# A recurrence unit in another order: the next unit's factors made first, the substitution split and moved ahead of the fifth level, three filler products removed

## What is computed

```python
def step(state, inp):                       # one head, one token
    r_t, w_t, k_t, v_t, kk_t, a_t = inp
    sa = einsum('bhij,bhj->bhi', state, -kk_t)
    state = (state * w_t[:, :, None, :] + sa[..., :, None] * (kk_t * a_t)[:, :, None, :]
             + v_t[..., :, None] * k_t[:, :, None, :])
    y = einsum('bhij,bhj->bhi', state, r_t)
    return state, y
```

## Time and profile before

| | |
|---|---|
| median of 3 runs | 1934.21 us (1932.78 to 1935.5) |
| the profiled execution | 1931.3 us, its span 1929.5 us |
| mean granted TensorE clock | 0.967 of full speed |
| TensorE matmuls busy | 1812.6 us, 94% of the span |
| VectorE, ScalarE, GpSimd busy | 676.8, 446.8, 71.6 us |
| the eight units, first z to the last unit's end | 228.22 to 498.60 us, 270.4 us |

### The profile page before, as it was taken

One profiled execution on the slowest core, in us unless ns is written; L12 is line 12 of the kernel. 1 busy time (PEld: TensorE's weight loads), 2 busy tenths in 40 slices (PEclk: granted clock), 3 DMA queues, 4 the chain that ended last, 5 costly groups with the idle time before them and its releaser, 6 DMA issues.

```text
span 1929.5 us, 22747 instructions
## 1 busy us (share of the span) xinstructions
PE 1812.6 (94%) x9052; PEld 880.3 (46%) x9052; DVE 676.8 (35%) x1285; ACT 446.8 (23%) x924; POOL 71.6 (4%) x110
## 2 busy tenths in 40 slices
PE   6999999999898999999999989778989999999998
PEld 3434478878554333333333344676543333333333
DVE  3159687776324111111111245673241111111114
ACT  3284323223421111111111132452111111111111
POOL 4130000000000000000000200000000000000001
PEclk9999899999998999999999999887989999999999
DMA  8000000001242999999999872100049999999997
GB/s 294 6 0 1 1 1 2 2 1 45 88 174 88 376 427 430 428 428 429 429 428 429 352 270 87 44 1 1 0 174 396 429 428 429 429 429 429 427 429 295
DMA packets 68230, 460.95 MB, mean 239 GB/s; under 512 B 18700, under 2 KB 19846, under 8 KB 43590
## 3 DMA queue, kind: packets, MB, share of 16 engines
q1 hardware_dynamic: 56118, 435.90, 54.4%
q10 hardware_dynamic: 9744, 15.77, 2.2%
q0 software_dynamic: 2304, 8.39, 1.3%
HBM read 442.21 MB, written 17.83 MB: 238 GB/s over the span
## 4 chain that ended last, share of the span: by engine, by line
PE 80%; DVE 10%; ACT 5%; issue 2%; DMA 2%; SPq 0%; POOL 0%; DVEq 0%; ACTq 0%; POOLq 0%
PE bank L713 21%; PE bank L739 12%; PE bank L687 11%; PE bank L1969 5%; PE bank L936 4%; PE bank L1015 3%; PE bank L2260 3%; PE bank L695 2%; ACT hT L459 2%; PE bank L2105 2%; PE bank L2114 1%; PE bank L2096 1%; PE bank L1001 1%; PE bank L273 1%; PE bank L1952 1%
## 5 line engine op out<-in xcount | busy, mean ns | idle before, releaser
L713 PE MATMUL bank<-ring,arena 128*64 128x512 f32 x2048 | 450.4, 592 | 1.6 <-DVE arena L539 1.6
L606 DVE TENSOR_TENSOR arena<-arena,bank 64x512 f32<-64x512 f32 x64 | 68.3, 1067 | 626.0 <-ACT arena L467 625.9
L713 PEld LDWEIGHTS bank<-ring,arena 128*64 128x64 f32 x2048 | 146.8, 137 | 293.4 <-issue 291.3
L687 PE MATMUL bank<-arena 128*64 128x512 f32 x1024 | 234.1, 599 | 7.3 <-DVE arena L606 4.9
L739 PE MATMUL bank<-ring,arena 128*64 128x512 f32 x1024 | 239.4, 610 | 0.9 <-ACT arena L471 0.9
L1969 PE MATMUL bank<-hT,ring 128*128 128x512 f32 x336 | 147.8, 600 | 5.7 <-ACT arena L1425 4.0
L687 PEld LDWEIGHTS bank<-arena 128*64 128x64 f32 x1024 | 73.8, 138 | 155.2 <-issue 128.8
L467 ACT ACTIVATE arena<-bank 64x512 f32<-64x512 f32 x64 | 37.9, 592 | 401.1 <-PE bank L713 401.1
L739 PEld LDWEIGHTS bank<-ring,arena 128*64 128x64 f32 x1024 | 69.2, 139 | 125.7 <-issue 124.5
L539 DVE TENSOR_TENSOR arena<-bank,gffn 128x512 f32<-128x512 f32 x64 | 44.3, 692 | 187.1 <-PE bank L695 187.1
L1969 PEld LDWEIGHTS bank<-hT,ring 128*128 128x128 f32 x336 | 64.3, 192 | 87.9 <-issue 87.9
(11 more groups left out here) (368 smaller groups left out, 1977.4 us busy)
## 6 DMA issues: line engine op xcount, KB each, us to landing
ring<-in_moe_w_gate_dram SPq DMA_DIRECT2D x64, 2048.0 KB, 10.3
ring<-in_moe_w_up_dram SPq DMA_DIRECT2D x64, 2048.0 KB, 15.0
ring<-in_moe_w_down_dram SPq DMA_DIRECT2D x64, 2048.0 KB, 12.5
expert_rows<-arena ACTq DMA_DIRECT2D x120, 128.0 KB, 8.2
ring<-in_rec_w_in_dram SPq DMA_DIRECT2D x5, 2048.0 KB, 12.8
ring<-in_att_w_in_dram SPq DMA_DIRECT2D x3, 2048.0 KB, 8.6
ring<-in_rec_w_out_dram SPq DMA_DIRECT2D x2, 2048.0 KB, 8.4
ring<-in_att_w_out_dram SPq DMA_DIRECT2D x2, 2048.0 KB, 19.2
```

The costliest lines, as they stand in the source:

```text
L606: nc.vector.tensor_tensor(hb[0:CAP, par, :].rearrange("s (f p) -> s p f", f=4), sg[0:CAP, par, :].rearrange("s (p f) -> s p f", f=4), bank ...
L687: mm = nc.tensor.matmul(bank[2][h * CAP:(h + 1) * CAP, :], onehot[:, par, t, :], xm[:, t, h * 512:(h + 1) * 512], start=(t == 0), stop=(t ...
L713: mm = nc.tensor.matmul(bank[par][k * CAP:(k + 1) * CAP, :], xg[:, par, c, :], W[k][:, c * FF:(c + 1) * FF], start=(c == 0), stop=(c == KC ...
```

## The change

The order of the steps inside a unit is another one on three engines. On TensorE `first_products` of the next unit comes after t 3 (in the place of rest 1), `spread_rows` after outputs 0 (in the place of rest 3), and rest 1, 2 and 3 come after z 4, rhs 1 and z 5. The filler products `spin(3, 0)` of each unit are gone. On VectorE parts 3 to 5 of `prepare` come straight after the masks of level 3; the next unit's masks, its masked M and its rows follow level 3's sums; `block_inverse` is split in `substitute`, after level 4's sums, and `blocks_out`, after level 5's masks. On ScalarE a new copy, `rows_copy`, takes the spread rows from bank 6 to SBUF (one 128x512 copy a unit), and the substitution reads them there; `exp_factors` of a unit is done at the end of the unit two before it (for unit 1 ahead of the first unit). The first unit's own factors are still made ahead of the loop, and the five filler products there stay. Unit 7 keeps its order. The semaphore `rhs_out` becomes `b6_out` and counts the new copies too.

```diff
@@ -219,8 +219,8 @@
...
-rhs_done, rhs_out, u_done, u_out, ys_done, ys_out, loop_step = (
-    sem(n) for n in ("rhs_done", "rhs_out", "u_done", "u_out", "ys_done", "ys_out", "loop_step"))
+rhs_done, b6_out, u_done, u_out, ys_done, ys_out, loop_step = (
+    sem(n) for n in ("rhs_done", "b6_out", "u_done", "u_out", "ys_done", "ys_out", "loop_step"))
@@ -345,6 +345,8 @@
...
+rows_n = lambda u: 3 * u - 3 if u > 1 else 1
+rhs_n = lambda u, s: 1 + 3 * u + (2 * s + 1 if u < UNITS - 2 else s + 1) - (u == UNITS - 1)
@@ -1469,7 +1471,11 @@
...
     def rhs_copy(ft, d, s):
...
-        nc.scalar.activation(RU[:, 0, :], bank[6][:, 0:256], ACT.Copy).then_inc(rhs_out, 1)
+        nc.scalar.activation(RU[:, 0, :], bank[6][:, 0:256], ACT.Copy).then_inc(b6_out, 1)
+
+    def rows_copy(u):
+        act.wait_ge(f_done, 3 * u + 3)
+        nc.scalar.activation(R8.rearrange("p k a j -> p (k a j)"), bank[6][:, :], ACT.Copy).then_inc(b6_out, 1)
...
     def u_copy(ft, d, s):
@@ -1535,14 +1541,14 @@
...
-        if u < UNITS - 1:
-            exp_factors((u + 1) // 2, (u + 1) % 2)
-        if u:
...
+        if u < UNITS - 1:
+            rows_copy(u + 1)
+        if u:
@@ -1550,6 +1556,8 @@
...
+        if u < UNITS - 2:
+            exp_factors((u + 2) // 2, (u + 2) % 2)
@@ -1557,6 +1565,7 @@
...
+    exp_factors(0, 1)
@@ -1796,24 +1805,32 @@
...
-        step(nc.vector.tensor_reduce(C8, bdm.rearrange("p a (b j) -> p a j b", j=8), AX.X, ALU.add))
-        nc.vector.tensor_tensor(R8, C8.unsqueeze(1).to_broadcast([P, 8, 8, 8]),
-                                E8.unsqueeze(2).unsqueeze(3).to_broadcast([P, 8, 8, 8]), ALU.mult).then_inc(f_out, 1)
...
     def first_products_out(u):
...
-    def block_inverse(u):
-        d, Tt = u % 2, Tb[u % 2]
+    def first_rows(u):
+        step(nc.vector.tensor_reduce(C8, bdm.rearrange("p a (b j) -> p a j b", j=8), AX.X, ALU.add))
+        nc.vector.tensor_tensor(R8, C8.unsqueeze(1).to_broadcast([P, 8, 8, 8]),
+                                E8.unsqueeze(2).unsqueeze(3).to_broadcast([P, 8, 8, 8]), ALU.mult).then_inc(f_out, 1)
+
+    def substitute(u):
+        d = u % 2
...
-        dve.wait_ge(f_done, 3 * u + 3)
+        if u:
+            dve.wait_ge(b6_out, rows_n(u))
+        else:
+            dve.wait_ge(f_done, 3)
...
-            row_ = m8(bank[6][:, k * 64:(k + 1) * 64])[:, :, js]
+            row_ = (R8[:, k, :, js] if u else m8(bank[6][:, k * 64:(k + 1) * 64])[:, :, js])
...
+
+    def blocks_out(u):
+        Tt = Tb[u % 2]
@@ -1876,31 +1893,42 @@
...
-        ready(0, 1, 2)
-        level_masks(u, 3)
-        rest_masks(u, 0)
-        ready(3)
-        level_sums(u, 3)
-        rest_masks(u, 1)
-        ready(4)
-        rest_masks(u, 2)
-        level_masks(u, 4)
-        ready(5)
-        rest_masks(u, 3)
-        level_sums(u, 4)
...
+            ready(0, 1, 2)
+            level_masks(u, 3)
+            ready(3, 4, 5)
+            rest_masks(u, 0)
+            level_sums(u, 3)
...
+            first_products_out(nxt)
+            first_rows(nxt)
+            level_masks(u, 4)
+            rest_masks(u, 1)
+            level_sums(u, 4)
+            substitute(nxt)
+            rest_masks(u, 2)
+            level_masks(u, 5)
+            blocks_out(nxt)
+            rest_masks(u, 3)
+            level_sums(u, 5)
...
+            level_masks(u, 3)
+            rest_masks(u, 0)
+            level_sums(u, 3)
+            rest_masks(u, 1)
+            rest_masks(u, 2)
+            level_masks(u, 4)
+            rest_masks(u, 3)
+            level_sums(u, 4)
...
-        level_masks(u, 5)
-        if nxt is not None:
-            first_products_out(nxt)
-            block_inverse(nxt)
-        level_sums(u, 5)
+            level_masks(u, 5)
+            level_sums(u, 5)
...
-    block_inverse(0)
+    first_rows(0)
+    substitute(0)
+    blocks_out(0)
@@ -2010,6 +2038,8 @@
...
+            if u < UNITS - 2:
+                pe.wait_ge(b6_out, rows_n(u + 2))
@@ -2024,7 +2054,7 @@
     def solve(ft, d, s):
...
-        pe.wait_ge(rhs_out, 2 * u + s + 1)
+        pe.wait_ge(b6_out, rhs_n(u, s))
@@ -2063,7 +2093,8 @@
...
     def first_products(u):
...
-        pe.wait_ge(m_out, 8 * u)
+        if u:
+            pe.wait_ge(m_out, 8 * (u - 1) + 2)
@@ -2072,12 +2103,14 @@
...
     def spread_rows(u):
-        pe.wait_ge(f_out, 3 * u + 1)
+        pe.wait_ge(f_out, 3 * u + 3)
...
     def turn_blocks(u):
-        pe.wait_ge(f_out, 3 * u + 3)
+        pe.wait_ge(f_out, 3 * u + 2)
+        if u:
+            pe.wait_ge(m_out, 8 * u)
@@ -2089,6 +2122,8 @@
...
+        if c == 1 and u < UNITS - 1:
+            pe.wait_ge(f_out, 3 * u + 5)
@@ -2185,20 +2220,29 @@
...
-        rest_products(u, 1)
+        if u < UNITS - 1:
+            first_products(u + 1)
+        else:
+            rest_products(u, 1)
...
-        rest_products(u, 2)
+        if u == UNITS - 1:
+            rest_products(u, 2)
...
+        if u < UNITS - 1:
+            rest_products(u, 1)
...
-        rest_products(u, 3)
+        if u < UNITS - 1:
+            spread_rows(u + 1)
+        else:
+            rest_products(u, 3)
...
-            first_products(u + 1)
+            rest_products(u, 2)
@@ -2207,16 +2251,15 @@
...
+        if u < UNITS - 1:
+            rest_products(u, 3)
...
-        if u < UNITS - 1:
-            spread_rows(u + 1)
-        else:
+        if u == UNITS - 1:
...
-            spin(3, 0)
...
```

## The result

The changed kernel takes 1910.54 us in the median of 4 runs (1908.86 to 1914.51); the kernel before, in 4 runs, 1934.54. The ratio is 0.988, with a 95% interval of 0.9862 to 0.9898: 24.0 us less (19.7 to 26.7), where 20 was forecast. The two profiled executions, with spans of 1907.5 and 1929.5 us, differ by 22.0.

A forecast was written before the change was run, and what follows sets the result against it. A unit was bound by TensorE up to first_products, then VectorE's chain, its wait covered by filler. Reaching TensorE's floor saves 3 x (3.43 + 3.22) = 19.95 us, rounded 20: 1934.2 to 1914.2 us, range 1908 to 1925.

The forecast's parts named there:

- The floor: Units 1 to 6: TensorE without filler and waits takes 31.27 (even) or 31.53 us (odd), 19.95 us less in all.
- The places on the clock: Unit 2's steps timed from its first z by swaps against the old timeline, first products at 8.61 us, for instance.
- The margins: Ready before wanted: rows 0.8 us, level 4's masks 0.55, rhs 1 0.4, rest 3 0.3, the unit's end level.
- the new waits: Four more waits a unit, already met: taken as costing nothing, with 2.4 us over six units kept for the range.
- Unit 0: First unit, VectorE busy 26.04 of 28.27 us: gain taken as nothing, between -2.2 and +2 us.
- The clock: TensorE's granted clock stays at 1.00 in each unit without the filler, the thin end being 2.1 us without a hole.
- the third case: Rival: without filler the clock falls once a unit, 2 us each, six times 12: 1926 us; chance 0.07.
- the second case: Rival: VectorE or ScalarE late at narrow places by 1 to 2.5 us a unit, 1920 to 1929 us; chance 0.13.
- The sum: Whole kernel: 19.95 us less, rounded 20, from the 1934.2 us median gives 1914.2 us.

The follow-up runs named there:

- The added operations: Changed kernel with VectorE's two first masks of each next unit done twice, 1.42 us more in its chain; 1918.08 us, ratio 0.9932 to the kernel before.
- The late substitution: Changed kernel with the substitution moved back behind level 5's masks, no filler; 1944.15 us, ratio 1.0063 to the kernel before.
- the late exponentials: Changed kernel with a unit's exponentials made in the middle of the unit ahead, as before the change; 1930.0 us, ratio 0.9985 to the kernel before.
- The two later comparisons: Unaltered changed kernel timed again beside the kernel before: 1909.97 us for 1931.45 (ratio 0.989), then 1911.73 us for 1932.55 (ratio 0.9898).

## Why the prediction was right, and where its sizes were off

The direction, the mechanism and the range held. Step by step:

- *The floor.* Forecast 31.27 and 31.53 us for even and odd units, measured 31.23 and 31.49 to 31.50. Over units 1 to 6 that is 20.18 us, for 19.95 forecast. That TensorE's own work is the floor is shown by the filler put back, which is paid in full; that VectorE's chain was the bound before is shown by the filler taken out of the old order, which leaves an idle TensorE.
- *The places on the clock.* Measured from z of unit 2: first products 8.61 (forecast 8.61), rows out 15.18 (15.1), masks of level 4 done 16.37 (16.29), t 4 at 16.71 (16.84), rhs 1 at 18.49 (18.7), substitution done 22.71 (23.25), rest 3 at 24.43 (24.6), last sums done 30.09 (30.14). Reading the old rows by swaps was good to 0.2 us, but for the substitution, done 0.54 sooner: W8 started 0.33 sooner (19.30, forecast 19.63), and took 0.18 in place of the 0.39 in the earlier trace rows. The 14 steps behind W8 take 3.19 us in both kernels, from the first, shown here (before, then after), to the group behind the last (at 322.32 before, at 310.13 after), so reading SBUF in place of PSUM changed nothing:

```profile
319.13 0.22 DVE L1815 TENSOR_TENSOR X<-bank,X 128x56 f32<-128x56 f32 x1
```

```profile
306.94 0.22 DVE L1829 TENSOR_TENSOR X<-X 128x56 f32<-128x56 f32 x1
```

- *The margins.* The rows had 0.57 us, not 0.8: spread_rows started 0.15 sooner than I reckoned, and the rows were out 0.08 later. The added operations bear out some 0.4 to 0.5. A margin was left out, that of the masked M ahead of rest 1; it measured 0.86 (done 299.96, wanted 300.82). Neither mattered, since nothing was late. That the new waits cost nothing where they are met came out too.
- *Unit 0.* Put at nothing, it won 0.86 us. The wait ahead of its first products, forecast at 2.5 us, is 2.30:

```profile
235.70 0.71 PE L2100 MATMUL bank<-ring 64*128 64x128 f32 x8 [2.30 <-DVE ring L1847]
```

- *The clock.* Forecast 1.00 in every unit, and so it is. The Trainium skill's rule in "TensorE: Matmul & The Clock Gate", Part 4, that transpositions don't count as busy in the same way, cost nothing here: turn_blocks (1.04 us; turn_last is in the code a plain product with an identity matrix) without filler, but also without a wait, leaves the clock at 1.00. The price of the third case was too low: a fall costs about 2.7 us in a unit of the old order without filler, where 2 stood in the forecast; that was worked out from one stretch of the earlier trace rows, and the fall there cost 1.7 us in all, not 1. The late substitution's unit 3 took 6.5 us more than an odd unit of the same order with filler (40.58 for 34.07). The waits of the second case, at 1.5 us and more, were priced without the clock; with the late exponentials waits of 1.7 to 2.6 us came with a clock below 1.00 in four of the units 1 to 6. The cases were not independent.
- *The sum.* 24.0 in the medians and 22.0 in the profiled pair, for 20. The units account for 20.18 + 0.86 of the pair, and unit 0 begins 0.29 later, together 20.75; the remaining 1.25 lie behind unit 7. There the kernel before lost 1.7 us to the fall of the clock in that execution, and the stages after that took 0.4 us less than in the changed kernel. This part is chance: repeated, the kernel before had no fall, and yet its time from unit 7's end to the end of the span was 1431.2 us for 1430.9, while three executions of the changed kernel have 1429.7 to 1434.8. The two later comparisons, with more runs, give 21.5 and 20.8 us by the medians, close to what the units won. So the 20 came out for the reason forecast, and unit 0 added 0.9.

## What to carry to other kernels

A filler that covers a wait is two things: time that a better order can win back, and a guard of the clock until it does. Take it out only together with the wait: alone it made the old order some 17 us slower, and one step put late in the new order (the substitution) lost the whole gain and more. To price a new order, put its steps on a clock by swaps against the old timeline and compare each pair of ready and wanted times; where margins are a few tenths, the place that is missed is more of a risk than the rows.

## What was not expected of the hardware

The same wait may or may not bring the clock down. With the late exponentials, unit 6 has the same wait ahead of its first products as unit 4, 2.61 us; unit 4 falls to 0.91 in the mean, and unit 6 stays at full clock:

```profile
442.94 1.16 PE L2100 MATMUL bank<-ring 64*128 64x128 f32 x16 [2.61 <-DVE ring L1847]
```

```profile
431.65:465.56 33.91, 31.20 (x312) 27.42 (x311) 25.64 (x53) 10.81 (x23) 1.45 (x2) 1.00 0.18 63
```

Unit 0 of the changed kernel keeps 1.00 through its 2.30 us; in the old order without filler each of the units 1 to 6, with 2.4 to 2.6 us and in five of them a second wait of 0.36 to 0.54 behind it, shows 0.91. Once it fell, the slow stretch ran through the next products, whatever their kind: z took 3.78 us for 2.05. What decides in a given unit stays open; no run here tried it apart.
